# Two of four weight sums per gate or up unit: from VectorE to adding DMAs issued by GpSimd

## What is computed

```
def swiglu(x, w_gate, w_up, w_down):
    return (jax.nn.silu(x @ w_gate) * (x @ w_up)) @ w_down

x = x + mixer(rmsnorm(x))
x = x + swiglu(rmsnorm(x), w_gate, w_up, w_down)     # w_gate, w_up 1024 x 2816, w_down 2816 x 1024
```

## Time and profile before

| | |
|---|---|
| median of three runs | 912.42 us (911.8 to 913.12) |
| the profiled execution | 912.69 us, its span 911.0 us |
| TensorE busy | 98% of the span, mean granted clock 0.99 |
| DVE, ACT, GpSimd busy | 65%, 40%, 29.5 us |
| ffn_1, from its first product to its last | about 520 to 657 us of the span |
| ffn_2 | about 729 to 836 us |
| HBM read | 80.65 MB |

### The profile page before, as it was taken

How to read it: one execution, slowest core, us unless ns; L and a number is a source line. 1 busy time by engine, 2 the same in 40 slices (tenths; PEclk the granted TensorE clock), 3 DMA queues, 4 the chain that set the end, 5 groups by cost and what they waited for, 6 DMA issues and landing times.

```text
span 911.0 us, 17815 instructions
## 1 busy us (share of the span) xinstructions
PE 892.0 (98%) x7009; PEld 886.7 (97%) x7009; DVE 591.5 (65%) x1135; ACT 363.3 (40%) x670; POOL 29.5 (3%) x47
## 2 busy tenths in 40 slices
PE   6999999999999999999999989999999999999996
PEld 6999999999999999999999989999999999999995
DVE  4567786657674443455557889999734489996454
ACT  7433222321334333222226556666511166664221
POOL 0000010000000000000000000000000000000330
PEclk8999999999999999999999989999999999999999
DMA  9312222222222222221222122222332223322302
GB/s 288 101 50 91 93 73 85 81 92 92 80 68 84 93 93 92 92 93 61 78 94 92 47 93 94 92 92 93 103 105 69 92 94 102 123 82 83 114 29 98
DMA packets 70524, 83.57 MB, mean 92 GB/s; under 512 B 1612, under 2 KB 66228, under 8 KB 67668
## 3 DMA queue, kind: packets, MB, share of 16 engines
q1 hardware_dynamic: 70484, 83.03, 27.8%
HBM read 80.65 MB, written 2.38 MB: 91 GB/s over the span
## 4 chain that ended last, share of the span: by engine, by line
PE 96%; DVE 1%; DMA 1%; ACT 1%; SPq 0%; issue 0%; DVEq 0%; ACTq 0%
PE ps_main L517 23%; PE ps_main L515 22%; PE ps_main L516 22%; PE ps_main L704 7%; PE ps_main L706 7%; PE ps_main L705 7%; PE ps_t L704 2%; PE ps_t L706 2%; PE ps_t L705 2%; DMA tok<-in_x_prompt_dram 1%; PE ps_g L636 1%; PE ps_t L547 1%; PE ps_g L547 0%; PE ps_g L637 0%; PE ps_main L769 0%; PE ps_main L770 0%
## 5 line engine op out<-in xcount | busy, mean ns | idle before, releaser
L515 PE MATMUL ps_main<-act_hi,w_hi 128*128 128x272 f32 x1612 | 467.2, 290 | 0.0
L517 PE MATMUL ps_main<-act_hi,w_lo 128*128 128x272 f32 x1612 | 467.0, 290 | 0.0
L516 PE MATMUL ps_main<-act_lo,w_hi 128*128 128x272 f32 x1612 | 464.2, 288 | 0.0
L515 PEld LDWEIGHTS ps_main<-act_hi,w_hi 128*128 128x128 f32 x1612 | 304.2, 189 | 0.8 <-issue 0.2
L516 PEld LDWEIGHTS ps_main<-act_lo,w_hi 128*128 128x128 f32 x1612 | 304.4, 189 | 0.2 <-issue 0.2
L517 PEld LDWEIGHTS ps_main<-act_hi,w_lo 128*128 128x128 f32 x1612 | 303.7, 188 | 0.0
L704 PE MATMUL ps_main<-xf_hi,w_hi 128*128 128x272 f32 x484 | 141.7, 293 | 3.0 <-ACT parts L931 3.0
L706 PE MATMUL ps_main<-xf_hi,w_lo 128*128 128x272 f32 x484 | 141.0, 291 | 0.0
L705 PE MATMUL ps_main<-xf_lo,w_hi 128*128 128x272 f32 x484 | 140.3, 290 | 0.0
L816 ACT ACTIVATE w_hi<-w_raw,g_cols 128x256 fp32r<-128x256 f32 x224 | 92.5, 496 | 97.4 <-PE ps_main L517 97.4
L1132 DVE SCALAR_TENSOR_TENSOR w_lo<-w_raw,g_cols,w_hi 128x256 fp32r<-128x256 f32 x224 | 91.3, 478 | 42.1 <-ACT w_hi L816 41.8
(11 more groups left out here) (214 smaller groups left out, 873.1 us busy)
## 6 DMA issues: line engine op xcount, KB each, us to landing
w_raw<-in_w_in_dram SPq DMA_DIRECT2D x27, 1024.0 KB, 5.0
w_raw<-in_w_gate_dram SPq DMA_DIRECT2D x11, 1024.0 KB, 4.8
w_raw<-in_w_up_dram SPq DMA_DIRECT2D x11, 1024.0 KB, 4.8
w_raw<-in_w_down_dram SPq DMA_DIRECT2D x8, 768.0 KB, 4.7
w_raw<-in_w_down_dram SPq DMA_DIRECT2D x8, 640.0 KB, 4.3
w_raw<-in_w_pa_dram SPq DMA_DIRECT2D x4, 1024.0 KB, 5.0
w_raw<-in_w_pb_dram SPq DMA_DIRECT2D x4, 1024.0 KB, 4.9
w_raw<-in_w_o_dram SPq DMA_DIRECT2D x4, 1024.0 KB, 4.9
```

The costliest lines, as they stand in the source:

```text
L515: pe.matmul(out, whi, xhi, start=(k == 0), stop=False)
L516: pe.matmul(out, whi, xlo, start=False, stop=False)
L517: last = pe.matmul(out, wlo, xhi, start=False, stop=(k == blocks - 1))
```

## The change

The sums 0 and 1 are not made by DVE any more. GpSimd issues, for each unit, a plain DMA of a quadrant from HBM into the sum's place in `w_sums` (B11 for sum 0, B12 for sum 1), and, when that has landed, a DMA that adds a second quadrant from HBM onto it (B12, B22). The load of all four quadrants into `w_raw` stays. ACT waits for the add's semaphore before forms 1 and 4, DVE waits for that of sum 0 before it makes sum 2. GpSimd's order for a unit q is: copy 0 once form 1 of unit q - 1 is split and its sum 2 made, copy 1 once form 4 of unit q - 1 is split, add 0, add 1. For unit 0 it starts when the mixer's buffers in that place are free.

```diff
-SUMS_BEFORE = {SUM_B11_B12: 1, SUM_B12_B22: 1, SUM_B11_B12_B22: 2, SUM_ALL: 3}
+SUMS_BEFORE = {SUM_B11_B12_B22: 1, SUM_ALL: 2}
+
+ADDED = {SUM_B11_B12: (B11, B12), SUM_B12_B22: (B12, B22)}
...
+        s_copied = [sem(f"s_copied{n}") for n in range(2)]
+        s_added = [sem(f"s_added{n}") for n in range(2)]
...
                 kind, n, _, _ = PRODUCTS[f]
                 if kind == "sum":
-                    act.wait_ge(w_summed, 3 * q + SUMS_BEFORE[n])
+                    if n in ADDED:
+                        act.wait_ge(s_added[n], 16 * q + 16)
+                    else:
+                        act.wait_ge(w_summed, 2 * q + SUMS_BEFORE[n])
...
             def sums_of_b(q, s, n):
 
                 raw = w_raw[:, s, :].rearrange("p (f n) -> p f n", f=4)
-                if n == 0:
+                if n == 1:
                     wait(dve, form_lo, NPROD * q)
-                    dve.tensor_tensor(w_sums[:, 0:2, :], raw[:, B11:B11 + 2, :], raw[:, B12:B12 + 2, :],
-                                      ALU.add).then_inc(w_summed, 1)
+                    dve.wait_ge(s_added[0], 16 * q + 16)
                 else:
-                    dve.wait_ge(w_summed, 3 * q + n)
-                    dve.tensor_tensor(w_sums[:, n + 1, :], w_sums[:, 0 if n == 1 else 2, :], raw[:, B22 if n == 1 else B21, :],
-                                      ALU.add).then_inc(w_summed, 1)
+                    dve.wait_ge(w_summed, 2 * q + 1)
+                dve.tensor_tensor(w_sums[:, n + 1, :], w_sums[:, 0 if n == 1 else 2, :], raw[:, B22 if n == 1 else B21, :],
+                                  ALU.add).then_inc(w_summed, 1)
...
             pool.memset(sq_sum[:], 0.0).then_inc(sum_done, 1)
 
+            def quad(q, n):
+                w = w_up if q % 2 else w_gate
+                return w[q // 2, :, n * QUAD:(n + 1) * QUAD]
+
+            def add_quads(q, n):
+
+                pool.wait_ge(s_copied[n], 16 * (q + 1))
+                pool.dma_start(w_sums[:, n, :], quad(q, ADDED[n][1]), accum_op=ALU.add).then_inc(s_added[n], 16)
+
+            pool.wait_ge(dve_out[1], p.taken[1])
+            pool.wait_ge(tile_half, 2 * p.tile(0, 0))
+            for q in range(Q1 + Q2):
+                if q:
+                    pool.wait_ge(form_lo, NPROD * (q - 1) + 2)
+                    pool.wait_ge(w_summed, 2 * (q - 1) + 1)
+                pool.dma_start(w_sums[:, 0, :], quad(q, ADDED[0][0])).then_inc(s_copied[0], 16)
+                if q:
+                    pool.wait_ge(form_lo, NPROD * (q - 1) + 5)
+                pool.dma_start(w_sums[:, 1, :], quad(q, ADDED[1][0])).then_inc(s_copied[1], 16)
+                add_quads(q, 0)
+                add_quads(q, 1)
+
             pool.wait_ge(form_used, NPROD * (Q1 + Q2))
```

More of the change, by code:

```diff
@@ L1466, in first_sums_of_b @@
                 quads_there(p, 0, 0)
-                for n in range(3):
+                for n in (1, 2):
                     sums_of_b(q, 0, n)
@@ L1544, in gate @@
                 quads_there(p, j, 1)
-                sums_of_b(q + 1, 1, 0)
                 form(q + 1, 1, 0)
@@ L1572, in up @@
                     quads_there(p, j + 1, 0)
-                    sums_of_b(q + 1, 0, 0)
                     form(q + 1, 0, 0)
```

## The result

| | before | after |
|---|---|---|
| median | 912.54 us (4 runs, 911.8 to 913.12) | 1012.65 us (4 runs, 1005.94 to 1013.63) |
| ratio | | 1.1088, 95% interval 1.1057 to 1.112 |
| span of the profiled run | 911.0 us | 1010.5 us |

The forecast was 921.6 us in a range up to 951. The direction was right; the size was wrong by a factor of eleven (9.2 us against 100).

A forecast was written before the change was run, and what follows sets the result against it. It took TensorE, busy for 98% of the span, as the bound; -0.3 + 2.8 + 2.5 + 3.3 + 0.9 gave +9.2 us on 912.69, so 921.9, 921.6 for the median, in a range from 913.6 to 951.

The forecast's parts named there:

- D = 5.3 us: Gate and up units: time from the end of form 4's split on DVE to add 0's landing, put at 5.3 us.
- 3.7, the 512 KB row: Term of D: add 0 lands in 3.7 us, like a 512 KB transfer, since it reads two operands of 256 KB.
- 0.9 for sharing: Term of D: 0.9 us more because add 0 shares the DMA engines with the w_raw load.
- the high end (9.1): Upper bound of D: the w_raw load gets ahead (4.8), then copy and add (3.6), and two issues: 9.1 us.
- Rival A: DMAs late for every unit, D = 6.8 and more: +38 us, 951 us at D = 6.8; chance 0.25.
- A round is 5.3 + D: Steady units: a round lasts 5.3 us plus D, slowing TensorE when over 10.59; 0.9 us counted over 18 units.
- D - 2.5: Start of the first stage, unit 0 to 1: TensorE's idle time grows by D - 2.5, counted as 2.8 us.
- D - 2.8: Start of the second stage, unit 12 to 13: TensorE is newly held for D - 2.8, counted as 2.5 us.
- -0.3 us: Gain from sparing DVE its 22 sums: the 0.3 us idle time of TensorE goes, counted as -0.3 us.
- one further fall: Start of the second stage: the new 2.5 us idle time of TensorE is followed by low clock, 3.3 us.
- What was hidden: Steady units: copies 0, copy 1 to add 1 (8.5 of 8.6 us) and the w_raw loads cost nothing.
- Copy 1's issue between form 4 and add 0 must be on the path: Sign expected in the changed profile: GpSimd issues copy 1 after form 4's split and ahead of add 0, delaying it.

The follow-up runs named there:

- e3: The changed kernel with the 1 MB load of a unit's quadrants held until add 0 has landed: 954.30 us.
- e9: The changed kernel with the load held until sum 0's second DMA has landed and second DMAs that copy, leaving out the second quadrant's addition: 934.97 us.
- e1: The changed kernel with add 0 issued right behind copy 0, copy 1 and add 1 staying where they were: 970.98 us.
- e2: The changed kernel with separate places for sums 0 and 1 of odd units, so all four DMAs go one unit earlier: 908.28 us, ratio 0.9951 to before.
- e8: Half of the change: only sum 0 by GpSimd's DMAs, sum 1 made by DVE just before form 3, one set of places: 908.90 us, ratio 0.9957.
- e4: The changed kernel with the second DMA of each pair copying in place of adding, which leaves out the second quadrant's addition: 978.85 us.
- e7: e2 with DVE also executing the spared 128x1024 sum at its old place, into a place written again before it is read: 911.18 us, ratio 0.998.

## Why the prediction was wrong

- **D = 5.3 us** is the step that failed. Measured 9.4 in the median, 6.4 to 9.8. Its parts: issues 0.7, measured 0.29 of notice + 0.55 for the copy, and add 0's own 0.9 inside its landing; "3.7, the 512 KB row" for the add, measured 4.5 in the median in e3, with the load held back; "0.9 for sharing", measured 4.0, the difference to the 8.5 of the changed kernel. So the sharing is the term that was mis-sized most. I had let the load and the small transfers share evenly. What happened is the order of the high end (9.1) that I worked out and passed over: where the load is issued within 0.5 us, it moves first and the add lands behind it. With the mean D of the steady units, 8.7, the forecast's own sum gives about 991. Rival A, at chance 0.25, was the right case.
- **"A round is 5.3 + D"** was right in form and short by about 1 us: 6.0 to 6.5 in three kernels. In e3 and e9 it is 5.7 and 6.2 in turn where nothing else waits. In the changed kernel every second one is 7.0: there product 4 has to be computed after ACT's late copy (at low clock 3.1 us, 591.58 to 594.67), then copied, before DVE can go on, which DVE's busy time alone leaves out. 18 units x (15.4 - 10.6) = 86 us, of which I had forecast 0.9; taken from the two traces, from split to split of form 4, it is 83.
- **The starts.** D - 2.5 and D - 2.8 with the measured D of 9.6 and 9.5 give 7.1 and 6.7 us; measured 7.0 (9.7 of idle time less 2.7) and 6.6. These two formulas hold. The -0.3 us is lost in the rest.
- **The clock.** I had one further fall, at the start of ffn_2, for 3.3 us. It came there (0.50 from 796 on), and it came in steady units as well: 28.3 us of additional busy time, here as at 592. The price was read a little low: 0.59 in 531 to 532 puts the fall at 531.2, so it lasts 6.8 us and costs 3.4.
- **What was hidden** stayed hidden: copies 0, the late w_raw loads (7.2 and 7.7 us to landing), and the second loop, copy 1 to add 1, which never set the end of form 4's split in the changed kernel, though it left nothing over in units 7, 11 and 19, where ACT's cast of form 4 starts 0.03 us or less behind add 1's landing.
- **The place in the order.** "Copy 1's issue between form 4 and add 0 must be on the path" holds by the chain, and e1 is worth 42 us. That the order is the root is shown by e2 and e8, where the same kinds of DMA run beside the kernel unnoticed.
- **D by a page's fit.** The 2.6 us that the Trainium skill, "DMA: Bandwidth & Descriptors", "Anatomy of one DMA — SWDGE (gpsimd) path", gives for 256 KB is less than any landing here, counted from the start of GpSimd's issue: the quickest plain copy took 3.2 (e4), 2.7 from the end of its issue. The Trainium skill's "Collectives: The Full Stack", "The bandwidth ceiling", puts ReduceScatter, whose add reads two sources, at about half the rate of AllGather, which only copies. The trace agrees for this add: 176 against 385 GB/s at full engines.

## To carry to other kernels

A DMA that takes over a compute step isn't free because its bytes fit: count from the moment its destination is released to its landing, in the company of the other transfers that the same moment releases, and compare that with the round. Here 88 DMAs cost 100 us or gave back 4, depending on whether they started behind the last use of the same buffer or one unit earlier. If a buffer's release lies on the round, give the DMA a second buffer (e2), or hand it only the part whose buffer is released early (e8). When a small transfer and a large load go out together, see which is issued first: a load 1.0 us or more behind cost add 0 less (5.6 to 6.9 us to landing, against 8.1 to 9.0), though no run changed that distance alone.

## What the hardware showed that I had not expected

- Transfers issued at nearly the same time didn't share evenly. A 256 KB add issued 0.3 us ahead of a 1 MB load landed after it, 8.07 us from its issue, where add 0 took 4.0 to 4.8 us in 18 of 22 units with the load held back (e3). With the load 1.0 to 1.2 us behind (changed kernel) it took 5.6 to 6.9, with the load 1.6 to 2.8 us behind (e8) 3.9 to 4.9. The load's own median rose from 4.8 to 7.2 and 7.7 us in the changed kernel.
- The adding form fills the engines for longer. GpSimd's queue took 11.6% of 1010.5 us for 88 DMAs of which 44 add, and 8.8% of 977.1 in e4, where none does: 117 against 86 us of all 16 engines. By subtraction an add of 256 KB takes 1.7 us of them, a plain copy 1.0; SP's queue (24.9% for 83.03 MB) takes 0.8 for 256 KB.
- In the changed kernel and in e4 GpSimd's issue took 0.54 to 0.57 us for nearly every plain DMA (0.7 for the first) and 0.87 to 0.92 for an add, SP's 0.33 to 0.35 for the load of a unit. In e1 and e2 a copy that starts while the add ahead of it is being issued took up to 0.90.
- An idle time of 2.7 us was followed by low clock in the kernel before and one of 2.6 was not in e7; which of the two happens was worth 2.5 us of TensorE's busy time. In the changed kernel one of 2.8 us (until 575.2) left the clock at 1.00, and in e1 one of 1.9 (until 781.7) was followed by 0.50: how long TensorE stands didn't settle it.
